# Scores of attention C: two heads' 64 plain rows on the array's two halves, the 32 position rows held twice and multiplied on four strips

## The chip, the cores and the metric
The program runs on one core of a Trainium2 chip. The metric is the device time of the whole program in microseconds; lower is better. A kernel's time is the median of several executions, and one more execution is recorded by the hardware profiler.

## The reference, cut to what matters
Two blocks follow each other on x of shape (1, 1024, 1024), all in fp32. The first (gated recurrences, state-space and attention-free branches, a feed-forward) is untouched. The second is two layers of attention: an even one (A: neighbourhood attention, B: full attention with rotary positions) and an odd one (C: latent attention, D: differential attention). The change is in C alone. It has 8 heads; a head's query and key have 64 plain dimensions and 32 position dimensions, which are rotated; the key's 32 are shared by all heads before their gain and norm:

```python
q = (rmsnorm_2(cq, g_cq) @ w_cq_b).reshape(B, S, H_C, C_NOPE + C_ROPE)      # 8 heads of 64 + 32
kv = (rmsnorm_2(ckv, g_ckv) @ w_ckv_b).reshape(B, S, H_C, C_NOPE + C_V)     # 64 + 64
k_nope, v_c = kv[..., :C_NOPE], kv[..., C_NOPE:]
k_pe = jnp.broadcast_to(kpe[:, :, None, :], (B, S, H_C, C_ROPE))
qc = rmsnorm_2(q, gq_c)
kc = rmsnorm_2(jnp.concatenate([k_nope, k_pe], -1), gk_c)
qc = jnp.concatenate([qc[..., :C_NOPE], rotate(qc[..., C_NOPE:], ang_mla)], -1)
kc = jnp.concatenate([kc[..., :C_NOPE], rotate(kc[..., C_NOPE:], ang_mla)], -1)
oc = attend_blocks(qc, kc, v_c, (C_NOPE + C_ROPE) ** -0.5)                  # softmax(q k^T scale) v
```

## The kernel before, in words
Everything is held with the feature on the partition and the token along the row: A(i) is one of 29 tiles of 128 partitions x 1024 tokens, PS is four PSUM tiles of 128 x 1024 fp32 (two banks each). TensorE's work is a list of jobs; each job takes the next PSUM tile in turn (`opn`, tile n % 4), waits until its last user has freed it (`freed`), and signals `filled`. So a job waits for the reader of the job four before it. There is no scheduler: each engine's block writes its own order by hand with generators. `weave(main, side)` takes one step of the main work (a unit of attention) and then one of the side work (projections of the heads to come).

**Attention C** (`attend_pairs("C", ...)`) has 32 units: 4 pairs of heads by 8 blocks of 128 queries. At step s TensorE does, in this order:
- the scores S of unit s, for the pair's heads m = 0 and 1 (L1270 to L1275): 96 rows of query and key, two matmuls of 512 keys for each head. A fp32 matmul shows as two records, so 8 records. Head 0's tile is waited for and filled before head 1's;
- O of unit s-2 (L1284): values by turned probabilities, the two heads side by side on the array's column halves, 32 records;
- T of unit s-1 (L1295): 16 transposes of the probabilities, into two PSUM tiles;
- then the side work's step. In this document X is the first job of it (or the next S, if there is none).

VectorE takes, for each head, the maximum of the score tile (L3306) and multiplies it by the row's scale (L2482 by its helper); then it gates O (L2474), and takes the reciprocals and scales the probabilities (L3326, L2478). ScalarE does the two exponentials straight from the score tiles (L2375, each followed by a read of its accumulator), which frees them, and copies T's two tiles out (L2385).

Attention B (L1257 to L1267) has 64-row heads and is written for the two halves: both tiles are waited for, and the matmuls go head 0, head 1, head 0, head 1, on rows 0 to 63 and 64 to 127. Attention A (L1214) multiplies 64 rows into 64 columns, four matmuls on the four quarters of the array.

**The side work of C** (`prep_c(h)`, four steps a head, heads 2 to 7 in units 0 to 23): (1) the query projection `qc` (8 records); (2) the sums for the query's norm (`hq`, L984), in heads 4 and 6 a gate projection of 48 records (L401), and the key projection `kc` (4 records of 64 columns); (3) the sums for the key's norm (`hn`, L480); (4) its spread over the partitions (`hb`, L503) and, for even h, the values. The last 8 units carry attention D's first head.

- ScalarE: `raw` (L1996, L1998) copies the query with its gain and squares it, and issues two DMAs that hold the 32 position rows turned by a half (L1990, L1991); in step (2) it copies the key's 64 rows (L2224), squares them (L2226), copies the shared 32 rows in from A(9) (L2229) and squares them from A(8) (L2231). The gates' SiLU needs a table load before and after (L2098, L1561).
- VectorE: `hq` (four small operations), then `rotate` (L3070 and on), three operations on 32 x 1024: turned rows by sine, rows by cosine, the sum. Later `hn` (a Newton step) and `kb`, the key by its norm.
- SyncE loads the weights in the order of the jobs into four slots; load w waits until the job of load w-4 is done (L1455 issues).

`prep_c0` (before the first unit) does the shared parts and heads 0 and 1 in the same way, with nothing over it.

## Time and profile before
| | |
|---|---|
| runs of the kernel before | 3873.71, 3878.88, 3873.5 us; median 3873.71 |
| the profiled execution's own time | 3871.55 us |
| its span, mean granted clock of TensorE | 3869.5 us, 0.984 |
| attention C, first S to last | 3017 to 3412 us |
| busy over the span: TensorE, weight loads, VectorE, ScalarE, GpSimd | 96%, 75%, 51%, 34%, 26% |
| chain that ended last, by engine | PE 82%, DVE 11%, ACT 4%, issue 3% |

How to read the rows. PE is TensorE, DVE is VectorE, ACT is ScalarE, SPq is SyncE's queue. A row names the line, the operation, out<-in, the shapes and how many (x8). In a timeline the first number is the start, the second the time from the first start to the last end; what stands in brackets is the idle time of the engine before, and what ended it. The chain of waits follows the end of the program back to what released each step. Matmul records overlap in their tails, so a length is best read from one start to the next.

### The profile page before, as it was taken

How to read it: one execution, taken by the hardware profiler on the slowest of the kernel's cores; microseconds unless marked ns; L12 is line 12 of the kernel's file. 1: busy time of each engine (PE TensorE's matmuls, PEld its weight loads, DVE VectorE, ACT ScalarE, POOL GpSimd, SP SyncE). 2: the span in 40 equal slices, each digit the busy share in tenths (PEclk: the TensorE clock that was granted, in tenths of full speed). 3: DMA queues.
4: the chain of work that ended last, by engine and by line, in shares of the span. 5: the costliest groups of instructions: out<-in, count | busy, mean ns of one | idle time of the engine just before them, and what ended most of it. 6: DMA issues, size and time to landing. Idle time of an engine off the chain costs nothing.

```text
span 3869.5 us, 51841 instructions
## 1 busy us (share of the span) xinstructions
PE 3706.4 (96%) x21561; PEld 2909.6 (75%) x21561; DVE 1985.1 (51%) x2505; ACT 1325.9 (34%) x1603; POOL 1018.0 (26%) x634
## 2 busy tenths in 40 slices
PE   8999999999999999999899999999999999999988
PEld 6778888878788887888788777666677566667767
DVE  8464455524652526333412556665754655456673
ACT  3243333322330112111201344455623666444450
POOL 4212222222233335666433411110022001111011
PEclk9999999999999999999999999999999999999999
DMA  4111111111125422222522211100121001111011
GB/s 146 34 50 50 44 53 47 50 44 47 55 79 182 147 88 66 86 83 82 195 78 70 85 43 43 44 17 9 53 66 54 14 13 27 31 25 25 17 55 68
DMA packets 283160, 238.56 MB, mean 62 GB/s; under 512 B 16976, under 2 KB 255728, under 8 KB 282928
## 3 DMA queue, kind: packets, MB, share of 16 engines
q1 hardware_dynamic: 262128, 166.04, 14.6%
q10 hardware_dynamic: 20800, 69.22, 5.0%
q8 instruction: 172, 2.82, 0.3%
q14 instruction: 60, 0.49, 0.0%
HBM read 181.81 MB, written 49.35 MB: 60 GB/s over the span
## 4 chain that ended last, share of the span: by engine, by line
PE 82%; DVE 11%; ACT 4%; issue 3%; POOL 1%; ACTq 0%; DMA 0%; DVEq 0%; SPq 0%; POOLq 0%
PE ps L401 19%; PE ps L418 18%; PE ps L451 15%; PE ps L902 9%; DVE AR L2474 3%; PE ps L1273 2%; DVE AR L2482 2%; DVE SM L3306 2%; PE ps L701 2%; PE ps L1284 1%; PE ps L1264 1%; PE ps L1295 1%; PE ps L503 1%; PE ps L1344 1%; PE ps L348 1%
## 5 line engine op out<-in xcount | busy, mean ns | idle before, releaser
L3439 POOL CAST WH<-WR 128x1024 fp32r<-128x1024 f32 (+2 forms) x231 | 240.8, 1043 | 2587.4 <-DMA WR<-in_w_in 827.1
L3441 POOL TENSOR_TENSOR WL<-WR,WH 128x1024 fp32r<-128x1024 f32 (+2 forms) x231 | 502.8, 2177 | 18.5
L2474 DVE TENSOR_TENSOR AR<-AR 128x512 f32<-128x512 f32 (+3 forms) x426 | 454.1, 1066 | 56.5 <-ACT AR L1822 38.1
L418 PE MATMUL ps<-ARR,WH 128*128 128x512 f32 x1472 | 367.1, 391 | 12.9 <-issue 10.7
L418 PEld LDWEIGHTS ps<-ARR,WH 128*128 128x128 f32 x1472 | 277.4, 189 | 71.6 <-issue 11.1
L401 PE MATMUL ps<-XH,WH 128*128 128x512 f32 (+2 forms) x1168 | 299.2, 399 | 4.6 <-POOL WL L3441 2.2
L401 PE MATMUL ps<-XH,WL 128*128 128x512 f32 (+2 forms) x1168 | 289.8, 390 | 0.0
L401 PE MATMUL ps<-XL,WH 128*128 128x512 f32 (+2 forms) x1168 | 288.6, 389 | 0.0
L401 PEld LDWEIGHTS ps<-XH,WH 128*128 128x128 f32 (+2 forms) x1168 | 215.9, 188 | 57.8 <-issue 8.0
L3306 DVE TENSOR_REDUCE SM<-ps 128x1 f32<-128x1024 f32 x128 | 156.8, 1225 | 197.3 <-PE ps L1273 116.1
L401 PEld LDWEIGHTS ps<-XH,WL 128*128 128x128 f32 (+2 forms) x1168 | 218.0, 187 | 48.8
L2474 DVE TENSOR_TENSOR H<-H,ps 128x1024 f32<-128x1024 f32 (+1 forms) x68 | 78.8, 1159 | 341.0 <-PE ps L418 340.7
L401 PEld LDWEIGHTS ps<-XL,WH 128*128 128x128 f32 (+2 forms) x1168 | 217.0, 186 | 48.0
L451 PE MATMUL ps<-XH,WH 128*128 128x512 f32 x864 | 236.5, 418 | 3.7 <-ACT AR L2315 2.3
L2482 DVE SCALAR_TENSOR_TENSOR AR<-ps,AR 128x512 f32<-128x512 f32 (+2 forms) x122 | 59.3, 486 | 341.5 <-ACT AR L1574 227.7
L2474 DVE TENSOR_TENSOR AR<-ps,AR 128x128 f32<-128x128 f32 (+2 forms) x193 | 102.1, 529 | 254.2 <-PE ps L902 220.7
L451 PE MATMUL ps<-XH,WL 128*128 128x512 f32 x864 | 214.4, 390 | 0.0
L451 PE MATMUL ps<-XL,WH 128*128 128x512 f32 x864 | 213.4, 389 | 0.0
L451 PEld LDWEIGHTS ps<-XH,WH 128*128 128x128 f32 x864 | 161.1, 197 | 57.3 <-issue 19.9
L451 PEld LDWEIGHTS ps<-XH,WL 128*128 128x128 f32 x864 | 163.1, 189 | 35.1
L451 PEld LDWEIGHTS ps<-XL,WH 128*128 128x128 f32 x864 | 162.2, 188 | 33.7
L2375 ACT ACTIVATE AR<-ps,SM,AR 128x1024 f32<-128x1024 f32 x112 | 135.0, 1205 | 152.2 <-DVE SM L2482 145.9
(295 smaller groups left out, 6257.3 us busy)
## 6 DMA issues: line engine op xcount, KB each, us to landing
WR<-in_w_in SPq DMA_DIRECT2D x78, 512.0 KB, 3.8
gates<-AR ACTq DMA_DIRECT2D x54, 512.0 KB, 2.8
AR<-gates SPq DMA_DIRECT2D x54, 512.0 KB, 4.3
H<-spill ACTq DMA_DIRECT2D x32, 512.0 KB, 5.9
WR<-in_w_in_e SPq DMA_DIRECT2D x26, 512.0 KB, 3.8
spill<-H ACTq DMA_DIRECT2D x24, 512.0 KB, 2.7
WR<-in_w_ffn_in SPq DMA_DIRECT2D x24, 512.0 KB, 3.8
WR<-in_w_in_o SPq DMA_DIRECT2D x23, 512.0 KB, 3.9
```

Source lines behind the costliest of these rows:

```text
L401: mm = pe.matmul(pt[0:m, h * 512:h * 512 + 512], wp[:, slot, k, 0:m], xp[:, k, h * 512:h * 512 + 512], start=i == 0, stop=i == 3 * KD - 1)
L418: mm = pe.matmul(pt[:, h * 512:h * 512 + 512], wp[:, w % 4, k, :], xp(k)[:, h * 512:h * 512 + 512], start=i == 0, stop=i == 3 * nk - 1)
L451: mm = pe.matmul(pt[:, h * 512:h * 512 + 512], wp[:, w % 4, k, :], xp[:, k, h * 512:h * 512 + 512], start=i == 0, stop=i == 3 * KD - 1)
L701: mm = pe.matmul(out, x1[r, c], later, start=True, stop=True)
L902: mm = pe.matmul(out, wp(i, slot)[:, 4 * half + k, :], xp(k), start=first and n == 0, stop=n == 11, skip_group_check=True)
L1273: mm = pe.matmul(pt[:, h * 512:h * 512 + 512], q(p, m)[0:96, rows], k(p, m)[0:96, h * 512:h * 512 + 512], start=True, stop=True)
L2375: act.activation(PROB[kind][i], PS[bank(("S", b, m))][:, :], ACT.Exp, scale=row_scale(kind, s, m), bias=SM[:, 20 + i:21 + i], accum_out=SM ...
L2474: return v.tensor_tensor(o, x, y, op)
L2482: return v.scalar_tensor_tensor(out=o, in0=x, scalar=s, in1=y, op0=op0, op1=op1)
L3306: v.tensor_reduce(SM[:, 34 + m:35 + m], PS[bank(("S", b, m))][:, :], AX.X, ALU.max)\
L3439: pool.tensor_copy(hi, full).then_inc(s_whi, 1)
L3441: pool.tensor_tensor(lo, full, hi, ALU.subtract).then_inc(s_wsplit, 1)
```

## The change
1. Scores of C: both tiles are waited for first; then four matmuls of the 64 plain rows (head 0 on partitions 0 to 63, head 1 on 64 to 127), then four of the 32 position rows, each on a strip of 32 partitions of its own: head 0's two halves of the keys on 64 to 95 and 96 to 127, head 1's on 0 to 31 and 32 to 63. The second four add to the first four's sums.
2. For that an odd head keeps its 64 plain rows on 64 to 127, and every head has its 32 position rows twice. The odd head's query projection has 128 columns, the position columns twice, and its weights come by three DMAs; its key projection writes to partitions 64 to 127.
3. The rotation of a query does a fourth operation that writes the second copy (`again`). The shared key rows are copied twice by ScalarE. They are held in A(26) and A(25), rows 96 to 127, whose tables are loaded to row 95 only.
4. Gains, norm weights and rotation tables have a form for odd heads.

```diff
-            def gemm(name, src, rhs, m=P, kp=P, nk=8, dup=False):
+            def gemm(name, src, rhs, m=P, kp=P, nk=8, dup=False, at=0):
...
-                        mm = pe.matmul(pt[0:m, h * 512:h * 512 + 512], WR[0:kp, w % 4, k, 0:m],
+                        mm = pe.matmul(pt[at:at + m, h * 512:h * 512 + 512], WR[0:kp, w % 4, k, 0:m],
...
+            def query_c(h):
+                if h % 2:
+                    gemm(("qc", h), (cols(wcq, h * 96 + 64, 32, nk=2), cols(wcq, h * 96, 64, nk=2)),
+                         rhs=lambda k: A(18 + k), nk=2)
+                else:
+                    gemm(("qc", h), cols(wcq, h * 96, 96, nk=2), rhs=lambda k: A(18 + k), m=96, nk=2)
+
+            def key_c(h):
+                gemm(("kc", h), cols(wckv, h * 128, 64, nk=1), rhs=lambda k: A(28), m=64, nk=1, at=h % 2 * 64)
...
-                            for m in range(2):
-                                pt, n = opn(("S", b, m))
+                            two = [opn(("S", b, m)) for m in range(2)]
+                            for pt, n in two:
                                 pe.wait_ge(freed[n % 4], n // 4)
-                                for h in range(2):
-                                    mm = pe.matmul(pt[:, h * 512:h * 512 + 512], q(p, m)[0:96, rows],
-                                                   k(p, m)[0:96, h * 512:h * 512 + 512], start=True, stop=True)
-                                mm.then_inc(filled[n % 4], 1)
+                            for h in range(2):
+                                for m, (pt, n) in enumerate(two):
+                                    e = slice(m * 64, m * 64 + 64)
+                                    pe.matmul(pt[:, h * 512:h * 512 + 512], q(p, m)[e, rows],
+                                              k(p, m)[e, h * 512:h * 512 + 512], start=True, stop=False,
+                                              skip_group_check=True)
+                            for h in range(2):
+                                for m, (pt, n) in enumerate(two):
+                                    e = slice(64 - m * 64 + h * 32, 96 - m * 64 + h * 32)
+                                    mm = pe.matmul(pt[:, h * 512:h * 512 + 512], q(p, m)[e, rows],
+                                                   k(p, m)[e, h * 512:h * 512 + 512], start=False, stop=True,
+                                                   skip_group_check=True)
+                                    if h:
+                                        mm.then_inc(filled[n % 4], 1)
...
-                if isinstance(src, tuple):
+                if isinstance(src, tuple) and m == P:
+                    for c in (0, 32):
+                        sp.dma_start(dst[:, 0:nk, c:c + 32], src[0]).then_inc(s_half_in, 16)
+                    sp.wait_ge(s_half_in, 16 * (dups[0] + 2))
+                    dups[0] += 2
+                    src, dst = src[1], dst[:, 0:nk, 64:P]
...
             def tables(which):
-                act.dma_start(A(25), a["rope"][2 * which]).then_inc(s_tab_in, 16)
-                act.dma_start(A(26), a["rope"][2 * which + 1]).then_inc(s_tab_in, 16)
+                rows = slice(0, 96 if which == 1 else P)
+                act.dma_start(A(25)[rows, :], a["rope"][2 * which][rows, :]).then_inc(s_tab_in, 16)
+                act.dma_start(A(26)[rows, :], a["rope"][2 * which + 1][rows, :]).then_inc(s_tab_in, 16)
...
             def shared_key(h, square):
-                act.activation(A(CK[h % 4])[64:96, :], A(9)[96:128, :], ACT.Copy).then_inc(s_act_step, 1)
+                for r in (0, 32):
+                    act.activation(A(CK[h % 4])[shared_at(h) + r:shared_at(h) + r + 32, :], A(26)[96:128, :], ACT.Copy)\
+                        .then_inc(s_act_step, 1)
+                    act.wait_ge(s_act_step, tick(s_act_step))
...
-                act.activation(kt[64:96, :], A(9)[96:128, :], ACT.Copy).then_inc(s_act_step, 1)
-                act.wait_ge(s_act_step, tick(s_act_step))
-                act.activation(A(22)[64:96, :], A(8)[96:128, :], ACT.Square).then_inc(s_kraw, 1)
+                for g in (c, c + 32):
+                    act.activation(kt[g:g + 32, :], A(26)[96:128, :], ACT.Copy).then_inc(s_act_step, 1)
+                    act.wait_ge(s_act_step, tick(s_act_step))
+                act.activation(A(22)[c:c + 32, :], A(25)[96:128, :], ACT.Square).then_inc(s_kraw, 1)
...
-            def rotate(x, tmp, ndma, rows=slice(0, P), i=0):
+            def rotate(x, tmp, ndma, rows=slice(0, P), i=0, again=None):
...
                 TT(x[rows, :], x[rows, :], A(25)[rows, :], ALU.mult).then_inc(s_dve_step, 1)
                 v.wait_ge(s_dve_step, tick(s_dve_step))
+                if again is not None:
+                    TT(x[again, :], x[rows, :], tmp[rows, :], ALU.add).then_inc(s_dve_step, 1)
+                    v.wait_ge(s_dve_step, tick(s_dve_step))
                 TT(x[rows, :], x[rows, :], tmp[rows, :], ALU.add).then_inc(s_rope_tmp, 1)
...
-                rotate(A(CQ[0]), A(27), 2, slice(64, 96))
+                rotate(A(CQ[0]), A(27), 2, slice(64, 96), 0, slice(96, P))
                 hq(RS[1], 96 ** -0.5)
-                rotate(A(CQ[1]), MSKF, 2, slice(64, 96), 1)
+                rotate(A(CQ[1]), MSKF, 2, slice(0, 32), 1, slice(32, 64))
...
-                rotate(A(CQ[h % 4]), A(27), 2, slice(64, 96))
+                rotate(A(CQ[h % 4]), A(27), 2, *((slice(0, 32), 0, slice(32, 64)) if h % 2 else (slice(64, 96), 0, slice(96, P))))
```

## Rows read from the trace of the kernel before

**Rows 1.** The page, part 1: TensorE's busy time, share of the span, instructions.

```profile
PE 3706.4 (96%) x21561; PEld 2909.6 (75%) x21561; DVE 1985.1 (51%) x2505; ACT 1325.9 (34%) x1603; POOL 1018.0 (26%) x634
```

**Rows 2.** Groups of instructions, 3015 to 3412: busy us, mean ns | idle before.

```profile
L3306 DVE TENSOR_REDUCE SM<-ps 128x1 f32<-128x1024 f32 x64 | 78.4, 1225 | 116.7 <-PE ps L1273 116.1
```

**Rows 3.** Chain of waits, the unit at 3143: start, us, what.

```profile
3143.33 3.63 PE ps L1273 x8
3146.96 1.90 PE ps L1284 x32
3148.86 1.90 PE ps L1295 x16
3150.76 1.09 PE ps L503 x16
```

**Rows 4.** Timeline, the unit at 3111, behind a projection.

```profile
3111.31 3.60 PE L1273 MATMUL ps<-AR 96*128 96x512 f32 x8
...
3113.30 1.22 DVE L3306 TENSOR_REDUCE SM<-ps 128x1 f32<-128x1024 f32 x1 [4.78 <-PE ps L1273]
...
3115.01 1.22 DVE L3306 TENSOR_REDUCE SM<-ps 128x1 f32<-128x1024 f32 x1 [0.30 <-PE ps L1273]
...
3116.55 1.21 ACT L2375 ACTIVATE MSK<-ps,SM,AR 128x1024 f32<-128x1024 f32 x1 [0.21 <-DVE SM L2482]
...
3118.54 1.84 PE L984 MATMUL ps<-CST,AR 96*128 96x2 f32 x16
```

**Rows 5.** Timeline, attention B, a unit without side work.

```profile
2580.30 1.99 PE L1264 MATMUL ps<-AR 64*128 64x512 f32 x8 [0.30 <-ACT AR L2375]
...
2582.39 1.23 DVE L3306 TENSOR_REDUCE SM<-ps 128x1 f32<-128x1024 f32 x1 [1.09 <-PE ps L1264]
...
2585.38 1.21 ACT L2375 ACTIVATE AR<-ps,SM,AR 128x1024 f32<-128x1024 f32 x1 [0.16 <-DVE SM L2482]
...
2586.72 1.99 PE L1264 MATMUL ps<-AR 64*128 64x512 f32 x8 [0.30 <-ACT AR L2375]
```

**Rows 6.** Timeline of TensorE, attention A's scores on four quarters, and what follows.

```profile
2255.14 1.09 PE L1214 MATMUL ps<-AR 64*64 64x512 f32 x8
2256.16 1.15 PE L1233 MATMUL ps<-AR 128*64 128x64 f32 x32
```

**Rows 7.** Timeline, the unit at 3176: the rotation of head 5.

```profile
3175.79 3.72 DVE L2474 TENSOR_TENSOR AR<-AR 32x1024 f32<-32x1024 f32 x3
3176.00 3.70 PE L1273 MATMUL ps<-AR 96*128 96x512 f32 x8
...
3179.54 1.23 DVE L3306 TENSOR_REDUCE SM<-ps 128x1 f32<-128x1024 f32 x1
...
3183.97 1.09 PE L480 MATMUL ps<-AR,CST 96*64 96x128 f32 x16 [0.39 <-ACT AR L2375]
```

**Rows 8.** Timeline, the unit at 3133: head 4's key on ScalarE.

```profile
3138.38 1.05 ACT L2231 ACTIVATE AR<-AR 32x1024 f32<-32x1024 f32 x1
...
3139.47 1.21 ACT L2375 ACTIVATE AR<-ps,SM,AR 128x1024 f32<-128x1024 f32 x1
...
3142.24 1.09 PE L480 MATMUL ps<-AR,CST 96*64 96x128 f32 x16 [0.27 <-ACT AR L2375]
```

**Rows 9.** Timeline, the start of C.

```profile
2997.30 1.28 ACT L2098 ACT_TABLE_LOAD   x1 [3.25 <-PE ps L401]
...
3010.74 0.29 DVE L2482 SCALAR_TENSOR_TENSOR AR<-ps,AR 128x128 f32<-128x128 f32 x1
```

**Rows 10.** Timeline, the last unit of C (S at 3394.39): its first exponential.

```profile
3398.26 1.21 ACT L2375 ACTIVATE AR<-ps,SM,AR 128x1024 f32<-128x1024 f32 x1
```

**Rows 11.** Timeline of SyncE's queue, head 5's query weights.

```profile
3111.50 0.37 SPq L1455 DMA_DIRECT2D WR<-in_w_cq_b  x1
```

**Rows 12.** Chain of waits: head 4's gate projection, head 5's query projection.

```profile
3120.38 11.00 PE ps L401 x48
...
3161.86 3.43 PE ps L348 x8
```

More of the change, by code:

```diff
@@ L54 @@
 CE = CEPS2 + 1
-CW = {n: CE + 8 + i * 70 for i, n in enumerate(["w64", "w96", "w128", "w256", "w1024", "weps"])}
+CW = {n: CE + 8 + i * 70 for i, n in enumerate(["w64", "w96", "w128", "w256", "w1024", "weps", "w96_odd"])}
 NCST = CE + 8 + len(CW) * 70
@@ L2162, in prep_c0 @@
                 act.wait_ge(filled[bank(("kpe",))], turn(("kpe",)))
-                act.activation(A(8)[96:128, :], PS[bank(("kpe",))][0:32, :], ACT.Copy)\
+                act.activation(A(25)[96:128, :], PS[bank(("kpe",))][0:32, :], ACT.Copy)\
                     .then_inc(s_act_step, 1)
@@ L2176, in prep_c0 @@
                 raw(("qc", 0), A(CQ[0]), A(22), 96, par("gqc", 0, 96), (A(27), (64,), 16, s_rot_in[0]))
-                raw(("qc", 1), A(CQ[1]), A(24), 96, par("gqc", 0, 96), (MSKF, (64,), 16, s_rot_in[1]))
-                act.activation(A(9)[96:128, :], A(21)[64:96, :], ACT.Copy).then_inc(s_act_step, 1)
+                raw(("qc", 1), A(CQ[1]), A(24), P, par("gqc_odd"), (MSKF, (0,), 16, s_rot_in[1]))
+                act.activation(A(26)[96:128, :], A(21)[64:96, :], ACT.Copy).then_inc(s_act_step, 1)
                 act.wait_ge(s_act_step, tick(s_act_step))
@@ L2213, in prep_c @@
                 act.wait_ge(s_rope_tmp, 6 + h)
-                raw(("qc", h), A(CQ[h % 4]), A(22), 96, par("gqc", 0, 96), (A(27), (64,), 16, s_rot_in[0]))
+                if h % 2:
+                    raw(("qc", h), A(CQ[h % 4]), A(22), P, par("gqc_odd"), (A(27), (0,), 16, s_rot_in[0]))
+                else:
+                    raw(("qc", h), A(CQ[h % 4]), A(22), 96, par("gqc", 0, 96), (A(27), (64,), 16, s_rot_in[0]))
                 yield
@@ L3120, in prep_c0 @@
                 for h in range(2):
[L3121 removed]
+                    kb(A(CK[h]), P, ("hb", cnt["hn"] - 2 + h))
                 yield
@@ L3130, in prep_c @@
                 yield
-                kb(A(CK[h % 4]), 96)
+                kb(A(CK[h % 4]))
                 yield
@@ L3481, in constants @@
         cst[:min(n, P), CW[f"w{n}"] + 6:CW[f"w{n}"] + 8] = 1.0 / n
+    for r in (slice(0, 32), slice(64, P)):
+        cst[r, CW["w96_odd"] + 6:CW["w96_odd"] + 8] = 1.0 / 96
     cst[:, CW["weps"] + 6:CW["weps"] + 8] = EPS / 1024
@@ L3520, in constants @@
     table(0, "pB", [(b + o, 16, ang) for b in (0, 64) for o, ang in ((0, row), (32, col))])
-    table(1, "pC", [(64, 16, angles(t, 32, 10000.0))])
+    table(1, "pC", [(b, 16, angles(t, 32, 10000.0)) for b in (0, 64)])
     part = angles(t, 16, 500000.0)
@@ L3563, in pack @@
     put("gkc", g("gk_c_2")[0])
+    for k, n in (("gqc_odd", "gq_c_2"), ("gkc_odd", "gk_c_2")):
+        put(k, np.concatenate([g(n)[0][64:], g(n)[0][64:], g(n)[0][:64]]))
     put("gsub", g("g_sub_d_2")[0])
```

44 lines of the change are left out of this document (26 added, 18 removed).

## Prediction

> **What bounds the kernel now.** The page first: TensorE is busy for 96% of the span [rows 1], which says nothing yet of the stage that changes. Attention C lies between 3017 and 3412 us of 3869.5. The groups of that stretch show VectorE idle for 116.1 us in wait for the scores [rows 2]: somebody waits for somebody in each unit, so I ask who waits last.
>
> A unit is one query block of two heads. TensorE does its scores S (8 matmul records of 512 columns), the output O of the unit before the last (32 records) and the transposes T of the last unit (16), then side work, which I call X. In the chain of the stretch a unit is all TensorE: S starts at 3143.33, O at 3146.96, T at 3148.86, X at 3150.76 [rows 3]. From S to X it is 7.43 us; where S follows a projection it is 7.23 (3111.31 to 3118.54) [rows 4]. It looks as if TensorE bounds the stage and S is its largest item.
>
> The second path is as long. VectorE takes the maxima of the two score tiles one after the other, ScalarE then both exponentials, and X uses the PSUM tile of the second head's scores (tiles are handed out in turn, S0 S1 O T0 T1 X, X is four after S1). So X waits for the second exponential. In [rows 4] the first maximum starts 1.99 us after S, because head 0's half of S is complete by then; the second 3.70 after; the second exponential starts 5.24 after and is over, with its accumulator read (some 0.2), at about 6.6. Slack: some 0.5 us before X.
>
> Attention B already has the shape that the change brings: both tiles waited for first, two heads on two halves, both complete at the end. There [rows 5] the maximum starts 2.09 us after S, the second exponential 5.08 after, and the next S, which stands where X does, 6.42 after, and it did wait for ScalarE. TensorE's own sum there is under 6: the chain sets the unit.
>
> **The scores, now.** 8 records of 64 rows, two at a time, are what B has. Then come 8 records of 32 rows on four strips. No row shows four row strips. The nearest is attention A, four matmuls on the four quarters of the array: 8 records of 512 columns from 2255.14 to 2256.16, 1.02 us [rows 6]. At 0.43 a record (3.43/8, [rows 12]) that is two turns of four, 0.86, and 0.16 for two changes of tiling, 0.08 each. B's S has its two changes already, the new one adds one: 0.86 + 0.08 = 0.94. Bounds: 0 if the strips ran beside the rest, and 8 x 0.43 = 3.44 if one at a time; I take 0.94 since attention A is the same number of matmuls side by side.
>
> The Trainium skill, "TensorE: Matmul & The Clock Gate", Part 3 (Measured speedup vs the span model), gives 3.07 times for four row strips of 512 columns. By that, as an estimate, the 3.44 would become 1.12 instead of 0.94, some 4 us more over the stage; no run here shows it yet, and my sum goes by the row.
>
> **What the shorter S is worth.** TensorE's unit: B's S of about 1.92 + 0.94, O 1.90, T 1.90 is 6.7, from 7.43: 0.7 us freed, times 32 is 23 us, the face value. But head 0's scores are now complete only with head 1's, 1.99 becomes 2.09 + 0.94 = 3.03, and the whole chain stands behind it: X comes at 6.42 + 0.94 = 7.36. Against 7.23 that is +0.13, against 7.43 it is -0.07. Of the 32 units about 15 are of the first kind and 6 of the second (S behind the norm's sums): +2.0 and -0.4, **+1.6 us**. The 0.7 is turned into a wait for ScalarE's L2375. The first unit, with no O or T, gives 0.7 back and the last loses as much, since its first exponential has only 0.5 us of other cover (it starts at 3398.26, 3.9 after S) [rows 10]. Nothing.
>
> The other units hang on the preparation, and their price is there.
>
> **The second copy of the turned queries** adds a VectorE addition of 32x1024, 1.22 and 0.03 between: 1.25 us a head. In odd heads, and in head 2, the three operations of the rotation run from 3175.79 to 3179.5 and the first maximum starts right behind, at 3179.54, 3.54 after S [rows 7]; X waits for ScalarE (0.39). The new scores are there at 3.03, so the rotation still ends last and 1.25 is paid in full: heads 2, 3, 5 and 7, **+5.0 us**. In heads 4 and 6 a projection of 11 us [rows 12] lies over the rotation: nothing; if the cover went, 1.25 each.
>
> **The second copy of the shared key rows** adds one ScalarE copy, 1.05 and 0.04 between. In heads 4 and 6 ScalarE is late: the gate comes with two table loads behind the 11 us projection, the copies end at 3139.43, the exponential starts at 3139.47 though its bias is long ready, and X at 3142.24 waits for it [rows 8]. 1.09 each, **+2.2 us**. In heads 2, 3, 5 and 7 the copy ends before the later maximum lets the exponential go: nothing.
>
> **The start of C.** VectorE goes through both heads' rotations, and the key's Newton step starts right behind them at 3010.74, with no idle before it [rows 9]; everything to the first S hangs on it. Two additions: **+2.5 us**. The two more key copies on ScalarE fall into its idle 3.25 us before the gate at 2997.30 [rows 9] (2.2 of it): nothing.
>
> **Loads.** An odd head's query weights come by three transfers instead of one, and SyncE waits for the first two before the third, with the next loads behind it. The load leaves at 3111.50, the projection that uses it runs at 3161.86 [rows 11, 12]: 50 us of cover against a few. SyncE's queue has nothing else due; POOL's splits wait for later loads of the same queue, tens of us ahead too. The gain columns, 128 instead of 96 rows, the output at rows 64 to 127: same column counts, nothing. The tables are shorter by 32 rows: nothing. Units 25 to 27 hang on the rotations of attention D and don't change.
>
> **Sum**: 1.6 + 5.0 + 2.2 + 2.5 = 11.3 us. The profiled execution took 3871.55 (span 3869.5), so 3882.9 by its own time; the median of the runs is 3873.71, 2.2 above, so 3885. A measurement of this kernel tells 0.2%, 7.7 us, from nothing.
>
> **Rivals.**
> (a) TensorE gives the time back. Place: X of each regular unit. If X did not wait for the second exponential (because the tiles' order lets TensorE run past it), 21 units at -0.7 are -15, others -0.7 each at best, and with the added work hidden beside it -23: 3851. It decides when X starts at 6.7 after S. For it: 96% busy and the chain of [rows 3] all on TensorE. Against: B's unit, whose TensorE work is shorter and which waits for ScalarE every time. With the added work paid it is near -4, no change. 0.05 for the full gain, 0.07 for the half.
> (b) The added work hides: VectorE's and ScalarE's additions fall in gaps that the lengthened wait for the scores opens. Then only 1.6 remains, 3875. For it: the first maximum is due 1.04 us later than now. Against: 3.03 is below 3.54 in [rows 7], and the additions at the start of C have no scores beside them. 0.13.
> (c) The strips go two at a time: 4 x 0.43 instead of 2, 0.86 more in the chain of 21 units, +18, 3903. Four of one kind have been seen only as quarters, whose column halves each meet two row groups; four strips write all 128 columns' results into four banks at once. 0.11.
> (d) One at a time: 2.58 more in each, 54 us and more, 3942. 0.03.
> (e) The change doesn't do what it says, and S stays at 3.6: no sign in the diff; under 0.01, with (b).
>
> **Numbers.** The forecast has 0.61, between +6 and +17 by itself (0.86 or 1.02 or the page's 1.12 for the strips, one or the other addition hidden, a longer wait at the start of C). About a sixth of it lies under +7.7. Faster by over 0.2%: (a) in full and a piece of its half, 0.07. Within: the rest of that 0.05, (b) 0.13, the low part of the forecast 0.10, together 0.28. Slower: 0.65. The range takes in (b) and most of (c)'s way: 3874 to 3900; left out are (a), (d) and half of (c), 0.2.
>
> **What would show it.** Right: S to O down from 3.63 to about 2.9; the first maximum 3.0 after S instead of 2.0; X at 7.36 after S with an idle before it "<- ACT L2375" of 0.6 or 0.7; TensorE's busy time in the stage down by 20 us and the stage 11 longer; four additions where three stand in the rotation, and the maximum right behind them in odd heads. Wrong: X at 6.7 after S (a); S to O at 3.7 (c) or 5.4 (d); the first maximum of [rows 7]'s unit at or before 3.6 after S (b).

## The result, and the profile after

The changed kernel takes 3914.50 us (median of 3906.84, 3913.85, 3915.15 and 3924.78), against 3875.55 for the kernel before on the same chip: ratio 1.0102, interval 1.0081 to 1.0124. That is some 39 us slower, where 11 were forecast and 3900 was the top of the range. The forecast was **wrong in size** by more than a factor of three; its direction was right. The profiled execution took 3915.15 us with a span of 3913.2, so it is 43.7 us longer than the profiled one before.

The page of the kernel after, parts 1 and 4, to be held against [rows 1]:

```profile
PE 3717.5 (95%) x21817; PEld 2909.2 (74%) x21817; DVE 1996.0 (51%) x2513; ACT 1335.0 (34%) x1611; POOL 1018.7 (26%) x634
...
PE 79%; DVE 12%; ACT 4%; issue 3%; POOL 1%; DMA 0%; ACTq 0%; SPq 0%; DVEq 0%; POOLq 0%
```

TensorE has 256 records more, which are the eight of the strips in each of the 32 units, and it is 11 us busier in a kernel that was to relieve it. I cut both traces at the same places: the stretch from the last gate's table load to C's first scores, and from the first scores to the last. The busy time by windows, kernel before (columns: window, its length, busy us and instructions of PE, PEld, DVE, ACT, POOL, granted clock, DMA share, GB/s):

```profile
2997.30:3017.19 19.89, 16.49 (x115) 10.42 (x115) 12.89 (x22) 12.21 (x17) 0.00 (x0) 0.84 0.07 16
3017.19:3394.39 377.20, 362.63 (x2413) 244.33 (x2414) 209.64 (x357) 207.69 (x266) 30.61 (x18) 0.99 0.09 21
```

The same of the kernel after:

```profile
3000.54:3022.93 22.39, 17.58 (x115) 11.92 (x115) 15.31 (x24) 12.23 (x17) 0.00 (x0) 0.71 0.08 16
3022.93:3434.09 411.16, 368.08 (x2660) 238.83 (x2660) 220.46 (x363) 214.19 (x272) 30.52 (x18) 0.95 0.08 19
```

So: +2.50 at the start of C, +33.96 in C, and the rest of the 43.7 is 3.2 ahead of that and 4.0 behind the last S. What happens ahead of C differs from one execution to the next: the first S stands anywhere from 3009 to 3017 us in the profiles of kernels whose code up to there is the one of before, and from 3016 to 3031 with the code of after. C's own length is the better measure. Its granted clock fell from 0.99 to 0.95; at half speed that is (1 - 0.95) x 2 x 411 = 41 us of C at 1.2 GHz. Before, it was 11: 3017 to 3021 and 3045 to 3052, the second one here:

```profile
3044.90:3051.70 6.80, 6.80 (x17) 3.02 (x14) 2.62 (x6) 2.62 (x5) 0.00 (x0) 0.50 0.00 0
```

So the strips' relief is real but small (TensorE is busy for 8.21 us of the unit at 3203.96, and was for 8.58 of the same unit before, at 3185.00), and the 30 us more at half speed take more than that back: in C TensorE is busy 5.5 us longer.

**A regular unit** (one with no added copy in it and no split of weights over its bias operations) goes as forecast, 0.2 late. The timeline of the kernel after, the unit at 3182:

```profile
3182.39 1.99 PE L1286 MATMUL ps<-AR 64*128 64x512 f32 x8
...
3184.31 1.14 PE L1292 MATMUL ps<-AR 32*128 32x512 f32 x8
...
3185.38 1.97 PE L1305 MATMUL ps<-AR 128*64 128x128 f32 x32
3185.57 1.22 DVE L3354 TENSOR_REDUCE SM<-ps 128x1 f32<-128x1024 f32 x1 [6.70 <-PE ps L1292]
...
3187.28 2.31 PE L1316 MATMUL ps<-CST,AR 128*128 128x128 f32 x16
...
3189.99 1.92 PE L985 MATMUL ps<-CST,AR 128*128 128x2 f32 x16 [0.41 <-ACT MSK L2420]
```

Four strips do run side by side: 8 records from 3184.31 to 3185.38, 1.07 us, S to O 2.99 instead of 3.63. The first maximum starts 3.18 after S, and X 7.60 after S with TensorE waiting 0.41 for ScalarE's second exponential; another part of the freed time went into the transposes (2.31, where they took 1.97 before). The unit at 3053 has X at 7.60 too (3053.06 to 3060.66).

**A unit in which the next gate's weights are split** is another thing. Timeline, the unit at 3168:

```profile
3168.89 1.99 PE L1286 MATMUL ps<-AR 64*128 64x512 f32 x8
...
3172.91 1.04 POOL L3487 CAST WH<-WR 128x1024 fp32r<-128x1024 f32 x1 [101.76 <-DMA WR<-in_w_in_o]
3173.33 0.63 DVE L2527 SCALAR_TENSOR_TENSOR SM<-SM,AR 128x1 f32<-128x1 f32 x1
...
3174.03 2.35 POOL L3489 TENSOR_TENSOR WL<-WR,WH 128x1024 fp32r<-128x1024 f32 x1
...
3175.26 1.14 DVE L2527 SCALAR_TENSOR_TENSOR SM<-SM,AR 128x1 f32<-128x1 f32 x1
...
3176.52 1.21 ACT L2420 ACTIVATE AR<-ps,SM,AR 128x1024 f32<-128x1024 f32 x1 [1.14 <-DVE SM L2527]
...
3177.96 1.07 PE L469 MATMUL ps<-CST,AR 128*128 128x128 f32 x8 [1.37 <-ACT AR L2420]
```

GpSimd splits the weights of a gate into two parts, a cast and a subtraction. L2527 is the bias operation (L2482 before), the row's maximum times its scale, one column of 128. It takes 0.16 us when VectorE is alone. Here the first ends at 3173.96, as GpSimd's cast ends (3173.95), and the second at 3176.40, as its subtraction ends (3176.38). The second exponential waits 1.14 for it, and X comes 9.07 after S. C has nine such splits, and in the kernel after all nine hold up the second bias operation of a unit (1.14 or 1.15 each). The groups of instructions of C give the sum of all 64 of these operations, first the kernel before, then after (busy us, mean ns | idle before):

```profile
L2482 DVE SCALAR_TENSOR_TENSOR SM<-SM,AR 128x1 f32<-128x1 f32 x64 | 12.4, 194 | 2.2
```

```profile
L2527 DVE SCALAR_TENSOR_TENSOR SM<-SM,AR 128x1 f32<-128x1 f32 x64 | 25.0, 390 | 2.2
```

The Trainium skill says this too ("SBUF — State Buffer", 🔬 SBUF: two separate sides): a VectorE operation with two inputs in SBUF and a GpSimd operation that reads SBUF lock the same pair of ports, and the later one is blocked until the other is through. By that rule both ends should fall on GpSimd's ends, and the trace agrees to 0.02 us; the maximum at 3174.00, with one input in PSUM, keeps its 1.23 under the same subtraction.

**A unit of heads 4 and 6** has the third cost. Timeline, the unit at 3144 and the next:

```profile
3148.35 2.14 ACT L2274 ACTIVATE AR<-AR 32x1024 f32<-32x1024 f32 x2
...
3151.61 1.21 ACT L2420 ACTIVATE AR<-ps,SM,AR 128x1024 f32<-128x1024 f32 x1
...
3153.05 1.60 PE L1316 MATMUL ps<-CST,MSK 128*128 128x128 f32 x8 [2.85 <-ACT AR L2420]
...
3156.48 3.78 PE L1286 MATMUL ps<-AR 64*128 64x512 f32 x8
...
3160.20 1.14 PE L1292 MATMUL ps<-AR 32*128 32x512 f32 x8
```

and the granted clock of the next S, by windows:

```profile
3156.48:3160.20 3.72, 3.72 (x11) 1.18 (x9) 0.88 (x3) 0.68 (x2) 0.00 (x0) 0.50 0.00 0
```

There are the two key copies that were forecast. TensorE stands 2.85 us for the exponential behind them, and after that the granted clock is 0.50 (1.2 GHz): the 64-row part of the next S takes 3.72 instead of 1.92.

### The profile page after: what moved, and what is told of

It reads as the page before. It is cut to its first block, busy times and chain, and to the rows that moved or that the text cites. A ratio compares the mean times of both kernels' runs of the same rounds, so it can differ in the third digit from the quotient of the medians.

```text
span 3913.2 us, 52409 instructions
## 1 busy us (share of the span) xinstructions
PE 3717.5 (95%) x21817; PEld 2909.2 (74%) x21817; DVE 1996.0 (51%) x2513; ACT 1335.0 (34%) x1611; POOL 1018.7 (26%) x634
## 3 DMA queue, kind: packets, MB, share of 16 engines
q8 instruction: 174, 2.85, 0.3%
## 4 chain that ended last, share of the span: by engine, by line
PE 79%; DVE 12%; ACT 4%; issue 3%; POOL 1%; DMA 0%; ACTq 0%; SPq 0%; DVEq 0%; POOLq 0%
PE ps L402 19%; PE ps L419 17%; PE ps L452 15%; PE ps L903 9%; DVE SM L3354 3%; DVE AR L2519 3%; PE ps L702 2%; DVE AR L2527 2%; PE ps L1286 1%; PE ps L1275 1%; PE ps L504 1%; PE ps L1365 1%; PE ps L349 1%; DVE SM L2527 1%; PE ps L1375 1%
## 5 line engine op out<-in xcount | busy, mean ns | idle before, releaser
L3489 POOL TENSOR_TENSOR WL<-WR,WH 128x1024 fp32r<-128x1024 f32 (+2 forms) x231 | 502.4, 2175 | 18.5
L419 PEld LDWEIGHTS ps<-ARR,WH 128*128 128x128 f32 x1472 | 277.8, 189 | 72.2 <-issue 11.6
L2527 DVE SCALAR_TENSOR_TENSOR AR<-ps,AR 128x512 f32<-128x512 f32 (+2 forms) x122 | 59.3, 486 | 347.0 <-ACT AR L1601 232.3
```

The source lines that it names most:

```text
L419: mm = pe.matmul(pt[:, h * 512:h * 512 + 512], wp[:, w % 4, k, :], xp(k)[:, h * 512:h * 512 + 512], start=i == 0, stop=i == 3 * nk - 1)
L2527: return v.scalar_tensor_tensor(out=o, in0=x, scalar=s, in1=y, op0=op0, op1=op1)
L3489: pool.tensor_tensor(lo, full, hi, ALU.subtract).then_inc(s_wsplit, 1)
```

## The experiments

Each was timed in five rounds against the kernel before on the same chip. The kernel before had medians of 3870.54 (runs 1 to 4), 3872.27 (5 to 8) and 3873.56 us (9 to 12) in these sessions, so a time is to be read as its distance from its own session's kernel before, and two runs of different sessions are compared by these distances. "C" is the time from first S to last S in the one profiled execution, "bias" the sum of the 64 bias operations of C.

| run | us above the kernel before | C, us | granted clock in C | bias, us |
|---|---|---|---|---|
| kernel before | 0 | 377.20 | 0.99 | 12.4 |
| kernel after | 39.0 | 411.16 | 0.95 | 25.0 |
| 1 order of the scores, in before | 41.4 | 413.48 | 0.96 | 20.8 |
| 2 later split, in after | 31.0 | 398.97 | 0.96 | 10.2 |
| 3 no late copies, in after | 39.8 | 405.21 | 0.96 | 25.6 |
| 4 waits filled, in after | 34.0 | 398.73 | 0.99 | 24.6 |
| 5 both 2 and 4 | 24.5 | 391.11 | 0.99 | 10.2 |
| 6 copies, in before | 19.2 | 390.82 | 0.97 | 12.9 |
| 7 one more maximum, in before | 20.6 | 392.92 | 0.98 | 28.1 |
| 8 one more maximum, in after | 51.5 | 425.91 | 0.94 | 21.7 |
| 9 later split, in before | -0.4 | 379.87 | 0.98 | 10.2 |
| 10 side work first, in after | 85.9 | 455.78 | 0.92 | 18.5 |
| 11 both 10 and 2 | 77.5 | 455.70 | 0.91 | 10.2 |
| 12 side work first, in before | 34.0 | 404.03 | 0.96 | 11.9 |

The intervals of the ratios below reach 0.13 to 0.23% to either side, 5 to 9 us; in C, units that an edit does not touch repeat to some hundredths of a us where the clock is the same.

**1. The order of the scores alone, in the kernel before.** TensorE's work stays as it was; both scores are late, as after.

```diff
-                            for m in range(2):
-                                pt, n = opn(("S", b, m))
+                            two = [opn(("S", b, m)) for m in range(2)]
+                            for pt, n in two:
                                 pe.wait_ge(freed[n % 4], n // 4)
+                            for m in (1, 0):
+                                pt, n = two[m]
```

> The kernel before with one edit: both score tiles are waited for and head 1's four 96-row matmul records go before head 0's, so head 0's scores are complete with the last record instead of half way. No strips, no copies, the same TensorE work. Theory (the chain maximum, maximum, exponential, X bounds the unit once the first maximum starts late): S to O stays 3.6 us, the first maximum starts 3.7 after S instead of 1.99, X comes at 3.7 + 4.4 = 8.1 after S instead of 7.23 to 7.43, in some 20 units: 15 us slower, and up to 12 more where the bias operation now falls under GpSimd's weight split, so 3889 to 3903. Rival (TensorE's work bounds the unit): X stays at 7.2 to 7.4, the time within 3 us of before.

Measured: 3911.94 us, ratio 1.0103 (1.0084 to 1.0122), C 413.48. This one edit costs what the whole change costs. Timeline of this kernel, the unit at 3182:

```profile
3182.30 3.70 PE L1275 MATMUL ps<-AR 96*128 96x512 f32 x8
...
3186.10 1.22 DVE L3308 TENSOR_REDUCE SM<-ps 128x1 f32<-128x1024 f32 x1 [0.30 <-PE ps L1275]
...
3190.53 1.09 PE L480 MATMUL ps<-AR,CST 96*64 96x128 f32 x16 [0.39 <-ACT AR L2377]
```

X comes 8.23 after S, behind ScalarE, and the step from the first maximum to X is 4.43, as after (3185.57 to 3189.99 is 4.42). That the late first maximum sets the unit is shown. But the chain was to cost 15 and the bias operations up to 12 more, and the kernel lost 41 and lies above the range of 3889 to 3903: something else comes with lateness, in both kernels. The granted clock in C is 0.96 here too.

**2. GpSimd's split after the bias operations.** In the changed kernel, the split of a weight waits until the next unit's bias operations are done.

```diff
+                at_step.append(step[0])
...
+                    step[0] = s if kind == "C" and s < nu else None
...
                     pool.wait_ge(w_in[w % 4], 16 * (w // 4 + 1))
+                    u = at_step[w - 4] if w >= 4 else None
+                    if u is not None and u + 1 < 32:
...
+                        pool.wait_ge(s_negmax, 96 + 2 * (u + 2))
```

> The changed kernel with one edit: during attention C GpSimd starts the split of a weight only when the unit in whose time the load lands has had its two bias operations on VectorE. Theory (in the changed kernel the bias operations, now over 1 us later in the unit, fall under GpSimd's split and take 0.6 to 1.1 us instead of 0.16, on the chain): the 64 small operations of C fall from 25.0 us in sum to about 12.4, units with a split from 9.1 to 7.6 between S and X, the time 8 to 13 us shorter, 3902 to 3906. Rival (these lie in slack, the loss is elsewhere): the sum falls all the same, the time by under 3 us.

Measured: 3901.53 us, ratio 1.0071 (1.0054 to 1.0088), C 398.97. In C 12.2 us come back; by the times it is 8 us, by the ratios 12, and the ratios' intervals still touch. Eight units in which a split lay over the bias operations are 12.8 shorter together; the other changes, up and down, come with the clock. Timeline of this kernel, the unit that stood at 3168.89, then the bias operations' group:

```profile
3162.19 1.99 PE L1289 MATMUL ps<-AR 64*128 64x512 f32 x8
...
3168.08 0.16 DVE L2530 SCALAR_TENSOR_TENSOR SM<-SM,AR 128x1 f32<-128x1 f32 x1
...
3168.40 1.04 POOL L3494 CAST WH<-WR 128x1024 fp32r<-128x1024 f32 x1 [100.33 <-DVE SM L2530]
...
3169.80 1.06 PE L471 MATMUL ps<-CST,AR 128*128 128x128 f32 x8 [0.39 <-ACT AR L2423]
```

```profile
L2530 DVE SCALAR_TENSOR_TENSOR SM<-SM,AR 128x1 f32<-128x1 f32 x64 | 10.2, 160 | 2.2
```

X is back at 7.61 after S instead of 9.07, and the bias operations take the 10.2 us of 64 undisturbed ones.

**3. No second copies for heads 4 to 7.** In the changed kernel; this leaves out part of C's scores in its last 16 units, as their second strips multiply rows left over from earlier uses of the tiles.

```diff
-                for g in (c, c + 32):
+                for g in (c, c + 32) if h < 4 else (c,):
...
-                rotate(A(CQ[h % 4]), A(27), 2, *((slice(0, 32), 0, slice(32, 64)) if h % 2 else (slice(64, 96), 0, slice(96, P))))
+                rotate(A(CQ[h % 4]), A(27), 2, *((slice(0, 32), 0, slice(32, 64) if h < 4 else None) if h % 2 else (slice(64, 96), 0, slice(96, P) if h < 4 else None)))
```

> The changed kernel without the second copies in heads 4 to 7: no fourth operation in their rotation, no second copy of the shared key rows (the strips of the second half of the keys then multiply rows that were never brought up to date: part of the scores of C is left out). Theory: 1.25 us each in heads 5 and 7, 1.09 each in heads 4 and 6, 4.7 in all, and the low-clock stretches that follow TensorE's waits of 2.85 us in heads 4 and 6 go or shrink, up to 2 us each: 5 to 9 us shorter than the changed kernel. Rival (the copies hide in gaps): under 1 us.

Measured: 3910.30 us, ratio 1.0099 (1.0082 to 1.0116), C 405.21. The units of the key copies (heads 4 and 6) and those right behind them went from 12.3, 12.4, 12.1 and 12.8 us to 11.0, 11.4, 10.1 and 10.6. The units of the rotations of heads 5 and 7 went from 10.3 and 11.1 to 9.9 and 11.6, so the 1.25 each that was expected there isn't seen; what the clock does in these two was not separated. C is 6 shorter, within the 5 to 9 expected, but the time, 39.8 above the kernel before instead of 39.0, doesn't show it.

**4. TensorE kept busy in its waits.** Products of constants into the unused second half of a PSUM tile, one of 256 columns before and one behind the second transposes of a unit, and 3 to 5 before them in units with long waits.

```diff
+                        spare = pt
...
+                            if kind == "C" and m and 2 <= s < nu:
+                                filler(spare, 5 if s in (10, 18) else 3 if s in (2, 6, 14, 22, 25, 26, 27) else 1)
                             pe.wait_ge(s_probs, first + 2 * (s - 1) + m + 1)
...
+                        if kind == "C" and 2 <= s < nu:
+                            filler(spare, 1)
...
+            def filler(pt, times):
+                for _ in range(times):
+                    pe.matmul(pt[:, 512:768], IDENT, CST[:, 0:256], start=True, stop=True)
```

> The changed kernel with idle TensorE time filled: in each unit of C from the third on a 256-column matmul of constants between the two turned tiles and one after them, three or five instead of one in the units with long waits, written to the unused second bank of O's tile and read by nobody. Theory (the lengthened waits lower the granted clock, 1.2 instead of 2.4 GHz for 41 us of C in the changed kernel, none of it in the same units of before): the granted clock over C rises from 0.95 to 0.99, units that took 12.3 and 12.7 us come back to 10.5 to 11, the time 8 to 18 us shorter, 3896 to 3906. Rival (the clock costs nothing because the chain on VectorE and ScalarE bounds the units): the clock rises, the time stays or grows by up to 6 us by the added matmuls.

Measured: 3904.53 us, ratio 1.0081 (1.0064 to 1.0098). C by windows:

```profile
3016.43:3415.16 398.73, 381.37 (x2821) 255.40 (x2821) 220.18 (x363) 214.19 (x272) 30.55 (x18) 0.99 0.08 20
```

TensorE is given more to do and C is 12.4 shorter, with the granted clock back at 0.99, while the bias operations still take 24.6 us. So the clock's fall is a cost by itself, and it comes from TensorE's waits. The time is 5 us nearer to the kernel before (8 by the ratios), less than the interval; for this one the proof is C.

**5. Both of the last two edits.**

> The changed kernel with both edits of the second and fourth run: GpSimd's splits wait for the unit's bias operations, and TensorE's idle time in C is filled with constant matmuls. Theory (collision and clock are separate causes): first S to last S of C takes 411.2 us in the changed kernel, 399.0 and 398.7 with one edit each; with both 386 to 389, that is the 377.2 of before plus the copies (7) and the chain (3 to 5); the time 3881 to 3889 against 3870 to 3876 of before. Rival (both remove the same loss): 396 or more, 3897 or more.

Measured: 3896.81 us, ratio 1.0058 (1.0045 to 1.0072). C by windows:

```profile
3031.27:3422.38 391.11, 379.98 (x2820) 255.25 (x2820) 225.32 (x363) 214.06 (x272) 32.82 (x18) 0.99 0.09 20
```

20 of the 34 us of C are back, and the time is 14 us nearer to the kernel before, with intervals that no longer touch. The two gains, 12.2 and 12.4, add up but for 4.6 us that both runs win: with the collisions gone the waits are shorter too, and the granted clock in C rose to 0.96 in experiment 2. The **expectation missed**, C by 2 us and the time, 3881 to 3889, by 8; it lies between the theory and the rival, at the rival's edge in time.

This run shows C with collisions and lower clock out of the way, so it gives the prices of the rest, unit by unit against the kernel before. The 20 regular units (here with those whose split is now held back) are 0.31 to 0.58 us longer each, 8.8 in all. The rotations of heads 3 and 5 cost 1.27 each, the key copies of heads 4 and 6 cost 1.18 and 1.19, the rotations of heads 2 and 7 0.42 and 0.44, no more than a regular unit. The other five units give 0.7 back: 2.7 of it in the unit at 3045, which ran for nearly half its time at the lower clock in the kernel before. Together 13.9.

**6. The copies alone, in the kernel before.** The scores stay as they were; the fourth operation of the rotation and the second key copy are added, to rows that nothing reads.

```diff
+                if again is not None:
+                    TT(tmp[again, :], x[rows, :], tmp[rows, :], ALU.add).then_inc(s_dve_step, 1)
+                    v.wait_ge(s_dve_step, tick(s_dve_step))
...
-                act.activation(kt[64:96, :], A(9)[96:128, :], ACT.Copy).then_inc(s_act_step, 1)
-                act.wait_ge(s_act_step, tick(s_act_step))
+                for r in (64, 96):
+                    act.activation(kt[r:r + 32, :], A(9)[96:128, :], ACT.Copy).then_inc(s_act_step, 1)
+                    act.wait_ge(s_act_step, tick(s_act_step))
```

> The kernel before with only the added copies: a fourth operation in each head's rotation (written to rows 96 to 127 of the turned rows' tile, read by nobody) and a second ScalarE copy of the shared key rows. Scores as before. Theory: 2.5 us before the first S, 1.25 each in heads 2, 3, 5 and 7, 1.09 each in heads 4 and 6, 9.7 in all, and a few us of low clock where TensorE's waits of 1.1 to 1.8 us grow: 3881 to 3888 at a before of 3871. Rival (copies hide): within 2 us of before.

Measured: 3891.48 us, ratio 1.0047 (1.0033 to 1.0060), C 390.82, 13.6 more. By the times it is 18 to 19 where 9.7 was the forecast of the copies, and above the expected range. The rotations of heads 3 and 5 cost 1.25 each and the key copy of head 4 costs 1.08, as forecast; the bias operations were hardly touched (12.9 us); the granted clock of C fell to 0.97, and some units with a copy or near one are 1.7 to 2.9 longer (at 3099, 3230, 3242, 3277 and 3290).

**7 and 8. One more maximum on the path of the second head**, over 256 columns, 0.425 us, in the kernel before and in the changed one.

```diff
+                            if kind == "C" and m:
+                                v.tensor_reduce(SM[:, 34 + m:35 + m], PS[bank(("S", b, m))][:, 0:256], AX.X, ALU.max)\
+                                    .then_inc(s_dve_step, 1)
+                                v.wait_ge(s_dve_step, tick(s_dve_step))
```

> The kernel before with one added VectorE operation a unit of C: a maximum over 256 of the second head's 1024 scores ahead of the real one, its result overwritten; some 0.45 us on the way from the second head's scores to X. Theory (in the kernel before the chain has 0.5 us of slack in regular units): no more than 3 us in the 20 regular units; the seven units of C that hang on VectorE or ScalarE at most 0.47 each; 0 to 6 us slower. Rival (the chain bounds before as well): 0.47 in each of 32 units, 15 us slower.

> The changed kernel with the same added operation. Theory (here the chain has no slack): 0.47 in each of some 28 units, 10 to 15 us slower than the changed kernel, X at 8.0 after S instead of 7.55. Rival (TensorE's work or the clock bound the unit): under 4 us.

Measured: before 3892.85 us, ratio 1.0058 (1.0042 to 1.0073), C 392.92; after 3923.81 us, ratio 1.0131 (1.0118 to 1.0144), 51.5 above its kernel before where the changed kernel is 39.0 above, so 12.6 for the maximum, C 425.91. After, regular units without a projection went from 10.3 to 10.8 and X to 8.06 after S: all 0.45 is paid, there is no slack, as expected. Before, the **expectation missed**: most regular units hardly changed (10.3, 10.7 and 10.9), so the slack of 0.5 is there, and still 20 us were lost by the times, 15.7 in C. Seven units are 1.1 to 3.5 longer, 14.6 together, and six of these have a split. Timeline of the kernel of run 7:

```profile
3261.85 2.36 POOL L3445 TENSOR_TENSOR WL<-WR,WH 128x1024 fp32r<-128x1024 f32 x1
3261.97 2.25 DVE L2482 SCALAR_TENSOR_TENSOR SM<-SM,AR 128x1 f32<-128x1 f32 x1
...
3264.35 1.20 ACT L2375 ACTIVATE MSK<-ps,SM,AR 128x1024 f32<-128x1024 f32 x1 [2.77 <-DVE SM L2482]
...
3265.79 1.92 PE L984 MATMUL ps<-CST,AR 96*128 96x2 f32 x16 [1.84 <-ACT MSK L2375]
...
3267.63 3.32 PE L348 MATMUL ps<-AR,WR 128*64 128x512 f32 x4
```

All of it in five rows: 0.4 us of lateness puts the bias operation under the subtraction, it takes 2.25 instead of 0.16, TensorE waits 1.84, and the projection behind it runs at the lower clock (3.32 for what takes 1.93). The kernel before stands at the edge of this: in six of the nine units with a split the second bias operation meets the end of GpSimd's cast (0.25 to 0.37 instead of 0.16) and gets through ahead of the subtraction.

**9. The later split in the kernel before.** The edit of experiment 2.

> The kernel before, with GpSimd's splits of the next weight held back until the bias operations of the next unit are done, as in e2. Theory (the split costs the changed kernel time only because its bias operations come 1.2 us later and so lie under it): here the bias operations were nearly all clear of it (194 ns in the mean), so their sum falls from 12.4 to some 10 us and the kernel stays within 4 us of the one before. Rival (a later split is worth something by itself, in any kernel of this shape): 8 to 14 us faster, as e2 was against the changed kernel.

Measured: 3873.13 us, ratio 1.0004 (0.9990 to 1.0018), bias operations 10.2 us. The split's place is worth nothing where the bias operations are ahead of the subtraction, and 12 us of C where they are not. The rival is out.

**10, 11 and 12. The side work ahead of the transposes**, an attempt to use TensorE's freed 0.6 us: X before T in three of a head's four steps; in the changed kernel, with experiment 2's edit, and in the kernel before.

```diff
+                    early = kind == "C" and s < 24 and s % 4 != 1
+                    if early:
+                        yield
                     if 1 <= s < nu + 1:
...
-                    yield
+                    if not early:
+                        yield
```

> The changed kernel with the side work put between O and the transposes in three of a head's four steps (18 of the 32 units; the step with the key projection keeps its order). The work is the same. X then uses the PSUM tile that was emptied in the unit before, and the second tile of the transposes is the one that waits for the second exponential, 1.1 us and more later in TensorE's order. Theory (the changed kernel is bound by the chain to the tile's release, with TensorE idle before it): in the 18 units the wait moves behind X and the second transposes start at about 7.6 after S, 0.95 before the unit's end instead of 1.09 to 3.4 before it, so units with short side work gain about 0.1 and those with a projection up to 2; 5 to 15 us faster than the changed kernel. Rival (X needs ScalarE's or VectorE's preparation, which stands behind the exponentials in their queues, so that it waits there instead and TensorE's idle only changes its name): within 4 us, or slower by as much as the preparation is late, 10 us and more.

> e10 and e2 together. If the two causes are apart, e10's gain and e2's 13 us add, and the kernel comes to 3886 to 3896; to beat the kernel before it would need 3865 or less, which I don't expect. If e10 loses, its loss stays and e2's gain is made smaller or larger by where the bias operations then lie.

> The kernel before with the same move of the side work as e10. Theory: its TensorE does not wait for the tile in regular units (its 0.5 us of slack), so the order brings nothing there: within 5 us. If X then waits for its preparation, it is slower, by as much as e10's X does.

Measured: 3959.42 (ratio 1.0225, 1.0204 to 1.0246), 3951.03 (1.0202, 1.0179 to 1.0225) and 3907.60 (1.0092, 1.0071 to 1.0114). All slower. Runs 10 and 12 lie 86 and 34 us above the kernel before, so the move costs 47 us in the changed kernel and 34 in the one before; the rival (10 us and more) had the size. In the kernel before, the expectation (within 5 us) missed. Experiment 2's edit gives 8 us by the times here, less than the intervals, and nothing in C (455.78 and 455.70), so the gain expected of run 11 was missed as well. Timeline of run 10:

```profile
3176.78 1.09 PE L481 MATMUL ps<-AR,CST 96*64 96x128 f32 x16 [2.46 <-ACT AR L2280]
...
3183.00 3.60 PE L1286 MATMUL ps<-AR 64*128 64x512 f32 x8 [2.40 <-DVE AR L2531]
```

and the group of all first parts of S in C, with their waits:

```profile
L1286 PE MATMUL ps<-AR 64*128 64x512 f32 x249 | 80.5, 770 | 49.1 <-ACT AR L2029 21.6 <-DVE AR L2531 14.4 <-ACT AR L2058 7.6
```

In the units of heads 4 and 6, X now waits 2.46 for ScalarE's square of the shared key rows (L2280), as the rival said. But most of the loss is in the next S, 49.1 us of waits: it needs the tiles that the side work left, and ScalarE (L2029, the square of a query; L2058, the copy of a projection) and VectorE (L2531) read those late, behind the exponentials and the copies of T's tiles. In the kernel before I expected no difference and there were 34: there too an S waits 2.43 for ScalarE. No kernel of this study beats the one before.

## Why the prediction was wrong

- **The strips.** Right, four at a time; 1.07 us where 0.94 was taken. The term was a seventh too small. The figure of the Trainium skill ("TensorE: Matmul & The Clock Gate", Measured speedup vs the span model), 3.07 times, gave an estimate of 1.12: nearer than the row of attention A. Rivals (c) and (d) are out, and (a) too: X stands at 7.6 with the idle that was named, though of 0.39 to 0.41 instead of 0.6 or 0.7. Rival (b) is out as well: the first maximum of the unit at 3193 starts 4.78 after S.
- **The chain.** Right in kind. X was to stand 7.36 after S and stands at 7.51 to 7.74 in the regular units (strips 0.13; the rest lies between first maximum and X, 4.42 where attention B's unit [rows 5] had 4.33). The size was far off: +1.6 was forecast for the regular units together, and 20 of them are 8.8 us longer with everything else removed (experiment 5). X stands 6.7 us later in these 20 together; the other 2.1 lie behind X, 0.1 a unit, and were not traced. Experiment 1 confirms the mechanism without any strip.
- **The copies.** Right in kind, too dear in sum. The rotation shows four operations and the maximum right behind, X again with 0.39 of wait; timeline of the kernel after:

```profile
3193.49 4.96 DVE L2519 TENSOR_TENSOR AR<-AR 32x1024 f32<-32x1024 f32 x4
...
3198.48 1.23 DVE L3354 TENSOR_REDUCE SM<-ps 128x1 f32<-128x1024 f32 x1
...
3202.91 1.09 PE L481 MATMUL ps<-AR,CST 128*64 128x128 f32 x16 [0.39 <-ACT AR L2420]
```

  The two units of this kind, heads 3 and 5, are 1.27 and 1.26 longer, where 1.25 stood. Heads 2 and 7 were priced the same and are not: their units are 0.44 and 0.94 longer, and 0.42 and 0.44 in experiment 5. (The unit of head 7 was already 1.1 longer than its like in the kernel before, by a collision of the kind told below.) The key copies of heads 4 and 6 cost their 1.09 and 0.1 more in experiment 5; in the kernel after the units are 2.2 and 2.0 longer. So the copies' 7.2 was nearer to 5. What they also do to the clock (experiment 6) had no term.
- **The start of C.** Right: +2.5, and +2.50 by windows, table loads and all. That it fits to the hundredth is luck. The same stretch took 19.7 to 20.3 us in the five traces with the code of before, and 22.0 to 22.4 in the eight with that of after, 2.1 more in the mean.
- **The step that failed** is "What the shorter S is worth": the later maximum was followed only through its own chain (+1.6 us, a term that measured some 9) and taken to be harmless beside it. Two things happen beside it, worth 20 us of C together, and neither had a term. First, **the bias operations came 1.2 us later, and there GpSimd's split of the next gate's weights lies over them**; POOL was looked at under "Loads" only for whether its input comes in time, not for what VectorE does while it runs. The collision was there to be read in the kernel before, on an operation that has slack, the probability scaling of the same unit (2.08 us, and 0.75 for the second head). Its timeline:

```profile
3158.89 2.37 POOL L3441 TENSOR_TENSOR WL<-WR,WH 128x1024 fp32r<-128x1024 f32 x1
...
3159.72 2.08 DVE L2478 TENSOR_SCALAR AR<-AR,SM 128x1024 f32<-128x1024 f32 x1
```

  And once it lay on the bias operation itself, in the unit at 3270, where X then waited 1.39; these rows of the kernel before would have given both the mechanism and its price:

```profile
3275.74 2.37 POOL L3441 TENSOR_TENSOR WL<-WR,WH 128x1024 fp32r<-128x1024 f32 x1
...
3276.97 1.16 DVE L2482 SCALAR_TENSOR_TENSOR SM<-SM,AR 128x1 f32<-128x1 f32 x1
...
3279.68 1.09 PE L480 MATMUL ps<-AR,CST 96*64 96x128 f32 x16 [1.39 <-ACT AR L2375]
```

  Nor is the meeting chance: the cast starts 4.17 us after the unit's S before (3153.60 to 3157.77) and 4.02 after (3168.89 to 3172.91), since the load leaves as S begins (SyncE, 3153.79 and 3169.00). A bias operation that comes 1.2 us later in the unit meets the subtraction in all nine units. The collision costs 12 us of C (experiment 2), and is nothing without the lateness (experiment 9). Second, **the granted clock was taken as fixed.** The text turned 0.7 us of work in each unit into a wait and priced the wait at its length; with waits of up to 2.85 us in it, C's clock went from 0.99 to 0.95. Filled waits give 12 us of C back (experiment 4).
- **The accounts of C's +34.0**: collision and clock 20.0 together (12.2 and 12.4 by the runs that take away one); of the other 13.9, by experiment 5, 8.8 in the 20 regular units, 4.9 in the four units with a copy that shows, 0.9 in those of heads 2 and 7, and 0.7 given back in the other five. The result is 39 above the kernel before where 11 were forecast; the 20 without a term are most of that. How the 4.0 us behind the last S divide was not tried; the last unit's O runs at the lower clock (3.68 for 1.97) behind a wait of 3.46.

The order alone (experiment 1) costs as much as the change. There X stands 8.1 to 8.2 after S, here 7.6, so the strips brought X some 0.6 us earlier in a regular unit, and the copies and the clock that goes with them took about as much away. That is argued from these two runs; a kernel with strips and without copies that computes the same was not tried. Maxima over a part of the keys, which would have shortened VectorE's part of the chain, were not tried: an exponential against a maximum of some keys can overflow.

## What to carry to other kernels

Before a step is made to finish later, list what every other engine runs in the time it moves to, GpSimd above all: a one-column VectorE operation on the chain costs what is left of the GpSimd instruction it meets. When two heads are packed so that both results come at the end, the gain in TensorE's time is to be set against the first result's delay, and the wait that replaces the work is to be priced with the clock it leaves behind. A kernel that looks to have 0.5 us of slack in each unit can lose 20 us to 0.4 of delay (experiment 7), so try such a delay by itself before building the change.

## What the runs showed of the hardware that was not expected

- A VectorE operation on 128x1 with two inputs in SBUF took 0.16 us alone, and 0.63, 1.14 and 2.25 under GpSimd's cast or subtraction of 128x1024, each time to within 0.02 us of the end of GpSimd's instruction. A maximum out of PSUM was not slowed (1.23).
- Four strips of 32 rows, with four different PSUM banks as targets, run at the same time in fp32: 8 records of 512 columns in 1.07 us, where 8 records of 64 rows on two halves took 1.92 and 8 of 96 rows, one at a time, 3.63.
- A wait of 2.85 us of TensorE was followed by a granted clock of 0.50 (1.2 GHz) in the next scores (3.72 for 1.92), and products of constants in the waits kept the clock at 0.99 over the stage, where it had been 0.95; they were worth 12 us of C more than they cost.
- A VectorE scaling of 128x1024 by one column, 0.75 us alone, took 2.08 when it began under GpSimd's subtraction (3159.72 in the kernel before).
